# Differential attention: weight splits moved to the end of each slot, two units ahead instead of three

## What is computed

```python
def diff_attention_layer(x, k, v, norm_g, w_in, lam_qk, sub_g, w_out, lambda_init):
    qg = rms_norm(x, norm_g) @ w_in                      # q and gate, 8 heads of 128
    ...
    scores = einsum("bhiqd,bhikd->bhiqk", qb, k) * scale - slopes * dist
    probs = softmax(where(allowed, scores, -inf))
    weights = probs[:, :, 0] - lam * probs[:, :, 1]
    out = einsum("bhqk,bhke->bqhe", weights, v)
    ...
    out = rms_norm(out, sub_g) * (1.0 - lambda_init)
    return x + (out * silu(gate)) @ w_out
```

## Time and profile before

| what | value |
|---|---|
| median of three runs | 1965.65 us (1965.1 to 1967.33) |
| the profiled execution, its own time | 1965.32 us |
| its span in the trace | 1963.5 us |
| TensorE matmul busy | 1902.3 us, 97% of the span |
| VectorE, ScalarE, GpSimd busy | 63%, 47%, 20% |
| mean granted TensorE clock | 0.998 |
| slots of the changed part | from 1661.0 us (slot 0) to about 1951 us |

### The profile page before, as it was taken

How to read it: one execution, slowest core, us unless ns; L and a number is a source line. 1 busy time by engine, 2 the same in 40 slices (tenths; PEclk the granted TensorE clock), 3 DMA queues, 4 the chain that set the end, 5 groups by cost and what they waited for, 6 DMA issues and landing times.

```text
span 1963.5 us, 26966 instructions
## 1 busy us (share of the span) xinstructions
PE 1902.3 (97%) x9396; PEld 1532.6 (78%) x9396; DVE 1234.2 (63%) x1797; ACT 923.7 (47%) x1563; POOL 384.4 (20%) x252
## 2 busy tenths in 40 slices
PE   5999999999999999999999999999999999999997
PEld 3778788888888666788888887788888887777776
DVE  8954443343459787543343459888768866778763
ACT  4864432232335576532232334455555553466662
POOL 6942100000045000200000045033323325000002
PEclk9999999999999999999999999999999999999999
DMA  5213333333333211233333333222222222222222
GB/s 206 47 31 127 96 96 96 96 96 96 97 97 96 66 44 44 86 96 96 96 96 96 97 96 96 76 76 76 66 85 76 76 72 84 81 65 66 74 65 75
DMA packets 54522, 166.98 MB, mean 85 GB/s; under 512 B 13216, under 2 KB 13344, under 8 KB 53920
## 3 DMA queue, kind: packets, MB, share of 16 engines
q1 hardware_dynamic: 54432, 165.78, 27.9%
HBM read 161.30 MB, written 2.10 MB: 83 GB/s over the span
## 4 chain that ended last, share of the span: by engine, by line
PE 74%; DVE 14%; ACT 6%; issue 3%; DMA 1%; DVEq 0%; ACTq 0%; SPq 0%
PE bank L183 14%; PE bank L185 14%; PE bank L184 14%; PE bank L1581 4%; PE bank L1583 4%; PE bank L1582 4%; PE bank L2209 2%; PE bank L2211 2%; PE bank L2210 2%; ACT Sm L1396 1%; PE bank L1597 1%; DVE w_lo L203 1%; PE bank L1599 1%; PE bank L1598 1%; ACT w_hi L195 1%
## 5 line engine op out<-in xcount | busy, mean ns | idle before, releaser
L203 DVE TENSOR_TENSOR w_lo<-raw,w_hi 128x1024 fp32r<-128x1024 f32 x286 | 367.3, 1284 | 435.9 <-ACT w_hi L195 433.9
L195 ACT ACTIVATE w_hi<-raw 128x1024 fp32r<-128x1024 f32 x289 | 305.4, 1057 | 384.6 <-DMA raw<-in_w_dram 384.5
L183 PE MATMUL bank<-x1h,w_hi 128*128 128x512 f32 x680 | 266.1, 391 | 1.2 <-DVE x1l L218 1.2
L185 PE MATMUL bank<-x1h,w_lo 128*128 128x512 f32 x680 | 264.6, 389 | 0.0
L184 PE MATMUL bank<-x1l,w_hi 128*128 128x512 f32 x680 | 264.5, 389 | 0.0
L183 PE MATMUL bank<-x0h,w_hi 128*128 128x512 f32 x640 | 250.3, 391 | 0.0
L185 PE MATMUL bank<-x0h,w_lo 128*128 128x512 f32 x640 | 249.0, 389 | 0.0
L184 PE MATMUL bank<-x0l,w_hi 128*128 128x512 f32 x640 | 249.0, 389 | 0.0
L232 POOL TENSOR_TENSOR sq<-h 128x512 f32 (+1 forms) x46 | 60.5, 1316 | 762.1 <-DVEq L974 659.7
L1581 PE MATMUL bank<-x1h,w_hi 128*128 128x512 f32 x384 | 153.7, 400 | 0.6 <-DVE w_lo L203 0.3
L183 PEld LDWEIGHTS bank<-x1h,w_hi 128*128 128x128 f32 x680 | 127.7, 188 | 28.8 <-DVE x1l L218 1.6
(11 more groups left out here) (426 smaller groups left out, 3616.7 us busy)
## 6 DMA issues: line engine op xcount, KB each, us to landing
raw<-in_w_dram SPq DMA_DIRECT2D x289, 512.0 KB, 3.5
h<-in_xT_dram SPq DMA_DIRECT2D x1, 2048.0 KB, 12.8
Ur<-in_xu_dram SPq DMA_DIRECT2D x8, 256.0 KB, 2.6
out_dram<-h SPq DMA_DIRECT2D x8, 256.0 KB, 2.2
const<-in_const_dram SPq DMA_DIRECT2D x1, 1028.0 KB, 14.0
B_st<-in_B_dram SPq DMA_DIRECT2D x1, 1024.0 KB, 7.4
C_st<-in_C_dram SPq DMA_DIRECT2D x1, 1024.0 KB, 14.8
p_in<-in_pT_dram SPq DMA_DIRECT2D x1, 1024.0 KB, 4.7
```

Of the source, the lines that this page charges most:

```text
L183: e.matmul(b, w_hi[:, w, k], xh[:, k], start=(k == 0), stop=False)
L185: last = e.matmul(b, w_lo[:, w, k], xh[:, k], start=False, stop=(k == KT - 1))
L195: e.activation(w_hi[:, z], raw[:, z], ACT.Copy).then_inc(hi_split, 1)
L203: e.tensor_tensor(w_lo[:, z], raw[:, z], w_hi[:, z].bitcast(F32), ALU.subtract).then_inc(w_split, 1)
```

## The change

The two splits behind the last Mamba slot are removed. In the differential attention slot n now splits unit U_KV2 + n + 2, and the split stands last in the slot on both engines: on VectorE behind the norm and the low halves of slots 0 to 3, on ScalarE behind the exponential of lambda (slot 1) and the silu of the gate (eight slots), ahead only of the squares of the end. Every unit is split once as before, and no instruction is added or removed.

```diff
@@ mamba_vector, behind the last slot
             evac(e, SLOTS - 1)
-            dve_split(e, U_MAMBA + SLOTS + LOADED, 0)
@@ mamba_scalar, behind the last slot
                 act_x(e, 8, 8, 6 + o, "kv2", x0h)
-            act_split(e, U_MAMBA + SLOTS + LOADED, 0)
@@ diff_vector, slot n
                     head_scales.took("rc", e.reciprocal(head_rg[:, H % 2], head_sd[:, H % 2]))
-                dve_split(e, U_KV2 + n + AHEAD, 0)
                 if n == 0:
                     dve_norm(e, 8)
                 if n < 4:
                     for m in (2 * n, 2 * n + 1):
                         dve_x(e, 9, m, "b_norm", x1h, x1l)
+                dve_split(e, U_KV2 + n + LOADED, 0)
@@ diff_scalar, slot n
                     head_scaled.took("k", last)
-                act_split(e, U_KV2 + n + AHEAD, 0)
                 if n == 1:
                     ...
                 if 0 < n <= HEAD_SLOTS and ORDER[n - 1][0] == "G":
                     j = ORDER[n - 1][1]
                     e.wait_ge(bank_free, evacuated2(n - 1))
                     gate_silued.took("g", e.activation(gate[:, j % 2], gate[:, j % 2], ACT.Silu))
+                act_split(e, U_KV2 + n + LOADED, 0)
                 if n > HEAD_SLOTS + 4:
                     ...
```

## The result

| | before | changed |
|---|---|---|
| median | 1965.59 us (6 runs) | 1976.87 us (6 runs, 1976.66 to 1978.24) |
| ratio | 1 | 1.0056, 95% interval 1.0046 to 1.0066 |
| profiled execution, time and span | 1965.32, 1963.5 us | 1977.84, 1976.0 us |
| mean granted TensorE clock | 0.998 | 0.995 |

The change costs 11.3 us; +10.3 was forecast, and 1976.87 lies in the range. So I compare slot starts against slot 0 of the same trace. In this trace slot 0 starts at 1662.09 instead of 1661.01.

A forecast was written before the change was run, and what follows sets the result against it. The prediction took TensorE, its matmuls busy 97% of the span, as the bound. Silu slots 10.3, start +1.05 and end −1.05 gave +10.3 us: 1965.3 + 10.3 = 1975.6 us, range 1971.0 to 1979.5.

The forecast's parts named there:

- `OT` later in slot 15: Behind slot 14's silu, `OT` waits for silu, split, `w_lo` and K in a row: 1.70 us later.
- start (slot 3): TensorE waits 1.5 us for `w_lo` at slot 2, and a 0.45 us wait for v goes: net +1.05 us.
- slot 10's silu (slot 13): `w_lo` comes 1.9 us later, but VectorE idled 1.46 us there before: +0.4 us.
- slot 14's (slots 16, 17): Silu ahead of the split in slot 14 delays VectorE's chain, for which TensorE already waited: +1.7 us.
- slot 22's (slot 24): Silu ahead of the split in slot 22, with 0.5 us of slack before the transposes: +1.2 us.
- slot 31's (slot 33): A second block directly follows slot 30's; TensorE starts slot 33 3.6 us late, 1.9 us more than slot 30's.
- end (slots 36 to 39): In slots 35 and 36 the split no longer waits for DMA and holds up `h`: about −1.05 us.
- the whole 1.70 us comes out on TensorE: Slot 15: TensorE already waited 0.67 us for the weights, so VectorE's 1.70 us delay reaches it in full.
- DMA waits: ScalarE's waits for DMA go; outside the last slots (3 to 6, 24, 28, 33) this is worth nothing.
- Absorbed: Rival: VectorE's idle time and its 54 us of waiting at `w_lo` swallow the delay, 1965.3 us; 7%.
- faster: Rival: without ScalarE's 22.6 us of DMA waits, all 5.2 us of TensorE's waits go, 1960.1 us; 3%.
- The dearer block: Rival: ScalarE's table load ahead of the split costs more than its row, +1.4 us in seven blocks, 1985 us; 4%.

The follow-up runs named there:

- e5: Changed kernel with unit U_KV2 + 2 split behind the last Mamba slot again and no split in slot 0: 1974.94 us, ratio 1.0040.
- e10: The kernel of e5 run once more, unaltered: 1975.23 us.
- e3: Changed kernel with ScalarE's split ahead of the silu in slot 14 alone: 1974.28 us, ratio 1.0044.
- e4: Changed kernel with ScalarE's split ahead of the silu in slot 18 alone: 1977.35 us, ratio 1.0060.
- e6: Kernel before with both splits two units ahead in their old places, without the two behind the last Mamba slot: 1964.75 us, ratio 0.9992.
- e2: Kernel before with only ScalarE's split moved behind the silu, still three units ahead: 1977.95 us, ratio 1.0061.
- e12: Kernel of e5 with ScalarE's split, still behind the silu, made of the unit three ahead; VectorE's stays two ahead: 1960.42 us, ratio 0.9972.
- e8: Changed kernel with ScalarE's split ahead of lambda's exponential and the silu, except in slot 14: 1969.96 us, ratio 1.0016.
- e11: The kernel of e8 run once more, unaltered: 1969.47 us.

## Why the prediction was right, and where a size was off

| step | forecast | trace |
|---|---|---|
| `OT` later in slot 15 | 1.70 | 1.69 |
| start (slot 3) | +1.05 | +0.92 |
| slot 10's silu (slot 13) | +0.4 | +0.4 |
| slot 14's (slots 16, 17) | +1.7 | +1.7, and 1.55 of clock |
| slot 18's (slot 20) | +1.7 | +1.67 |
| slot 22's (slot 24) | +1.2 | +1.21 |
| slot 26's (slot 28) | +1.7 | +1.66 |
| slot 30's (slot 32) | +1.7 | +1.67 |
| slot 31's (slot 33) | +1.9 | +1.84 |
| end (slots 36 to 39) | −1.05 | −1.22 |
| sum | +10.3 | +11.4 |

- **The one term that was mis-sized is that of slot 14.** The step "the whole 1.70 us comes out on TensorE" left out that a longer idle stretch can lower the clock behind it. Slots 16 and 17 together add 3.24 us; e5 and e10, with the same wait and no fall, add 1.68 to 1.69 us, so the remaining 1.55 us is the clock. In e3, with the short wait, both are gone. Without it the sum would be 9.9 us.
- **Slack read from one pair of rows held.** Slot 22's 0.5 us of slack gave 1.21 us, slot 10's idle 1.46 us gave 0.4.
- **Slots 31 to 33.** The size is right; the way was not quite the one described. In slot 32 the clock fell again, 0.65 us behind its first matmul (0.62 over 2.7 us from 1913.07), but its second half has to wait for G7's bank in any case, so the slow matmuls cost nothing there. e4 shows it, where the clock stayed at 1.00 in slot 32: TensorE waits 1.30 us for that bank, and from slot 31 to slot 33 it loses 3.56 us, as against 3.52 in the changed kernel.
- **Where the DMA waits went.** They were costed at nothing outside the last slots; e6 shows it: nothing until slot 35, 1.2 us between the starts of slots 35 and 38. They did not go to near zero as forecast: 6.1 us are left, of which 5.28 us is the wait for the last unit, 5.38 before. That wait has stayed, but the last unit's split now comes a slot later, so the `h` that stood behind it on VectorE stands ahead of it.
- **The rivals.** "Absorbed" and "faster" both rested on waits that TensorE does not see; the delay shrinks nowhere between slots 3 and 33, and e2 shows the silu order alone at +0.61%. The dearer block: the table load takes 1.28 us and follows 0.03 us behind the scaling in the changed kernel, so the 2.66 us for a switch in the Trainium skill ("ScalarE: Activation LUTs", What ACT_TABLE_LOAD costs) are not seen here either.
- **A count.** On each engine 38 splits move, of units U_KV2 + 2 to U_KV2 + 39, not 39; nothing in the sum rests on it.

## What to carry to other kernels

When work on one engine is waited for by another, the price of moving it is not its own lateness but that of all that stands behind the waiting instruction: look for what is queued behind `w_lo`, not for when `w_lo` is needed. Give such a pair a slot of distance: in e12 the place in the slot then cost nothing. And the total of a wait (54.2, 49.5 and 41.0 us at `w_lo` in kernels of 1965.6, 1976.9 and 1964.8 us) says little of what it costs. Where TensorE is the bound, each place has its own slack, to be read between two rows; here the losses of the places added up, and none came back.

## What the runs showed of the hardware that was not expected

TensorE's granted clock fell to 0.50 for some 3 us behind a wait of 2.3 us, after more than 1600 us at 1.00, and this cost 1.55 us, nearly as much as the wait's growth. It is no fixed price: six of nine such waits had it, and two runs of the same kernel (e5, e10; and e8, e11) agreed with each other. The fall in slot 32, behind two shorter waits, cost nothing, for TensorE had to wait there in any case. The Trainium skill ("TensorE: Matmul & The Clock Gate", Part 1: The HAM clock gate) has the two levels and says that the moment of the rise, once matmuls have begun, varies from run to run. The traces agree on the levels (1.00 and 0.50); what is said of the rise is not said of a fall behind a wait, and no run here shows what decided the fall.
